# Hybrid decoder layer: ScalarE's order in the stick task, the fields' layout and requests, and who splits values in two stages

## Chip, cores and metric

One NeuronCore of a Trainium2 chip runs the whole layer as one launch. The metric is the device time in microseconds (us); 1,000 ns are 1 us. TensorE multiplies matrices, VectorE, ScalarE and GpSimd work on elements, SyncE's queue (SP) issues most DMA requests. In rows of the profile they are PE (PEld for its weight loads), DVE, ACT, POOL and SP.

## The reference

For 16 learned tokens followed by 1,024 others, all 1,024 wide, one layer is computed:

```
xn = RMSNorm(h);  P = xn @ W_in
A:  RWKV-7, 8 heads x 64: token shift, decay, gates, the scan
    S = S * w + (S @ -kk) (kk * a)^T + v k^T,   y = S r,  group norm, bonus, gate
B:  stick-breaking attention, 8 heads x 64, for s < t:
    z = q.k / sqrt(64)
    log A[t,s] = log_sigmoid(z[t,s]) + sum over s < j < t of (log_sigmoid(z[t,j]) - z[t,j])
    o = A @ v, RMSNorm per head
h += RMSNorm(concat(A, B) @ W_out)
h += RMSNorm(relu(RMSNorm(h) @ W_up)^2 @ W_down)
```

Since log_sigmoid(z) - z = -softplus(z), an exponent in B is z minus a running sum of softplus(z) over the keys between.

## The kernel before

The layer runs as stages, one after the other, with a barrier between them: the norm and transpose of x, the input projection (`stage_in_proj`), the two mixers together (`stage_mix`), the heads' norms (`stage_post_heads`), the output projection, and the feed-forward part. The change touches the middle three.

**High and low halves.** A large product of float32 values is made of three (or, with one exact side, two) products in the rounded type fp32r. Each operand is split: the high half is the value converted to fp32r, the low half is the value minus the high half. Whoever makes the high half and whoever makes the low half are named in the code by `high...` and `low...`.

**`stage_in_proj`** also prepares five fields for each of the four pairs of RWKV heads, cut into 17 chunks of 64 tokens, and stores them to `chunk_dram`; `F_A`, `F_R`, `F_B`, `F_K`, `F_V` give their places there (places 0 to 4).

**`stage_mix`** runs two independent computations interleaved on the same engines. The RWKV scan goes by laps, one lap a chunk, 18 laps of 8 slots each (`LAP_SLOTS`): in lap n the front half of chunk n and the rear half of chunk n - 1. A chain of small products of TensorE alternates with steps of VectorE (masked copies out of PSUM: `nb`, `xx`, `krk`, `zi`, `fv`, `qm`, `state`) and copies of ScalarE (`xx`, `xt`, `wu`, `nb`, `fv`, `y`). The chunk's fields are loaded by `load(n, s)` into `fld` (A, R, an identity that stays, B) and, with the halves of the partitions exchanged, into `swp` (A, R, K, V): six requests a chunk on SP's queue.

The sticks go by ticks. There are 124: 112 tasks (four pairs of heads, two heads, two groups of 512 queries, blocks of 128 keys; 64 tasks are 512 columns wide, 16 each 384, 256 and 128) and 12 turns that transpose v. Each engine runs its own list, a tick is cut into four quarters on each, and `program` deals the quarters out behind the slots of the laps, evenly. Every engine executes in order, so a quarter that waits holds up all that stands behind it, the lap's steps too. For task t the work is:

- TensorE, tick t, quarter 0: z into the one PSUM bank `zb` (2 products), after ScalarE has copied the z of t - 1 out
- ScalarE, tick t, quarter 2: the copy of z to SBUF (L1026)
- VectorE, tick t, quarter 3: w = min(z, 40) (L1149)
- ScalarE, tick t + 1, quarter 0: w = exp(w), w = ln(1 + w) (L1011, L1013)
- VectorE, tick t + 1, quarter 2: the maximum of z and w, which is softplus (L1142)
- GpSimd: on the diagonal blocks a mask (L915), then the high half (L934) and the low half (L936)
- TensorE, tick t + 3, quarter 3: the running sum (`tri`, 2 products, or one for a narrow task)
- VectorE, tick t + 4, quarter 0: the exponent, z minus the sum (L1130)
- ScalarE, tick t + 5, quarter 1: exp of it, the weights (L1019); GpSimd masks them on the diagonal
- TensorE, ticks t + 5 and t + 6: `rest` (2 products) and the product of two heads' weights with v

The first requests of the stage are: v of pair 0, the six of chunk 0, q and k of pair 0 in four (part 0), the six of chunk 1, q and k in four more (part 1), v of pair 1. Before the first tick's end ScalarE needs part 0 and part 1 (`high_q`, `high_k`).

**`stage_post_heads`** takes the mean and variance of y over each head with TensorE (`ones_bd`), ScalarE makes 1/sqrt as exp(-0.5 ln), VectorE applies norm, bonus and gate for the four pairs, and then the norm of o. Beside it `w_out` is split for the next stage, eight tiles of 128x1024: high halves by VectorE (L1470) between the first norm step and the rest, low halves by GpSimd (L1490). Four of the tiles (`w_raw`) are already there, four (`w_rest`) are loaded in the stage, behind the bonus and gate of pair 0. Bonus and gate have two buffers: SP loads those of pair q once pair q - 2 is gated.

## Time and profile before

| | us |
|---|---|
| median of 3 timed runs (lowest to highest) | 1727.83 (1727.64 to 1730.01) |
| the profiled execution | 1725.34 |
| its span, first to last instruction | 1723.6 |
| PE, DVE, ACT, POOL busy in the span | 1566.2, 816.3, 696.6, 513.2 |
| stage_mix, first request to last instruction (378.4 to 840.5) | 462 |
| stage_post_heads (840.8 to 894.3) | 53 |

The first three lines measure the same kernel; the profiled execution lies 2.5 us under the median. Busy times are sums of the durations of an engine's instructions; in the sum for PE a product counts until its result has landed, so a PE that is shown busy isn't at its peak.

### The profile page before, as it was taken

What the parts mean: (1) busy time and instruction counts of PE and PEld (TensorE: products, weight loads), DVE (VectorE), ACT (ScalarE), POOL (GpSimd) and SP (SyncE); (2) the same over time, 40 slices, a digit from 0 to 9 for tenths busy, and PEclk for the clock granted to TensorE, in tenths of its full rate; (3) what the DMA queues carried; (4) which work ended last, traced back from release to release, by engine and by line L of the source; (5) the groups of instructions that cost most, each with busy time, mean ns of one, the idle gap of its engine ahead of it and who ended that gap; (6) DMA issues with size and microseconds to landing.
All of it is one profiled execution on the core that took longest, in us unless ns stands there. A gap on an engine that the chain in (4) does not pass through costs nothing. (4 is left out here: it accounts for less than half of the span.)

```text
span 1723.6 us, 38309 instructions
## 1 busy us (share of the span) xinstructions
PE 1566.2 (91%) x15700; PEld 1307.7 (76%) x15700; DVE 816.3 (47%) x1125; ACT 696.6 (40%) x1231; POOL 513.2 (30%) x523
## 2 busy tenths in 40 slices
PE   4999999976988889889919959999999999999997
PEld 3999999965676666767508848888888888888886
DVE  5133433324666667666663434444444444444436
ACT  5144534415777677667723432222222222222213
POOL 6432343322545355454533431111111111111110
PEclk7999999987999999999959979999999999999999
DMA  3334354463512323111331232111111111111104
GB/s 133 115 127 159 131 203 148 153 185 71 144 46 61 71 55 77 46 46 25 99 85 73 86 111 73 49 49 49 49 49 49 49 49 49 49 49 49 61 0 171
DMA packets 81570, 143.98 MB, mean 84 GB/s; under 512 B 15632, under 2 KB 51472, under 8 KB 81440
## 3 DMA queue, kind: packets, MB, share of 16 engines
q1 hardware_dynamic: 77696, 128.26, 24.3%
q10 hardware_dynamic: 3744, 13.85, 2.0%
q8 instruction: 99, 1.62, 0.4%
q14 instruction: 31, 0.25, 0.0%
HBM read 104.51 MB, written 37.57 MB: 82 GB/s over the span
## 5 line engine op out<-in xcount | busy, mean ns | idle before, releaser
L1816 POOL TENSOR_TENSOR ffn_ul<-ffn_relu,ffn_uh 128x512 fp32r<-128x512 f32 x64 | 82.8, 1294 | 575.8 <-ACT ffn_uh L1788 575.8
L1845 DVE TENSOR_TENSOR all_acc<-all_acc,ffn_down 128x512 f32<-128x512 f32 x240 | 161.1, 685 | 122.1 <-PE ffn_down L1892 121.5
L618 PE MATMUL inproj_acc<-xn_xh,inproj_wh 128*128 128x346 f32 (+1 forms) x624 | 207.6, 333 | 8.4 <-DVE inproj_wl L539 8.4
L1884 PE MATMUL ffn_up<-all_mh,ffn_wuh 128*128 128x512 f32 x512 | 200.2, 391 | 11.3 <-DVE ffn_wul L1828 11.3
L618 PE MATMUL inproj_acc<-xn_xh,inproj_wl 128*128 128x346 f32 (+1 forms) x624 | 201.2, 322 | 0.0
L618 PE MATMUL inproj_acc<-xn_xl,inproj_wh 128*128 128x346 f32 (+1 forms) x624 | 201.2, 322 | 0.0
L1892 PE MATMUL ffn_down<-ffn_wdh,ffn_uh 128*128 128x512 f32 x512 | 200.0, 391 | 0.0
L1884 PE MATMUL ffn_up<-all_ml,ffn_wuh 128*128 128x512 f32 x512 | 199.9, 390 | 0.0
L1884 PE MATMUL ffn_up<-all_mh,ffn_wul 128*128 128x512 f32 x512 | 199.9, 390 | 0.0
L1892 PE MATMUL ffn_down<-ffn_wdh,ffn_ul 128*128 128x512 f32 x512 | 199.4, 389 | 0.0
L1892 PE MATMUL ffn_down<-ffn_wdl,ffn_uh 128*128 128x512 f32 x512 | 199.2, 389 | 0.0
L1836 DVE TENSOR_TENSOR ffn_relu<-ffn_relu 128x512 f32<-128x512 f32 x64 | 44.3, 692 | 218.9 <-ACT ffn_relu L1786 218.9
L1780 ACT ACTIVATE ffn_wdh<-ffn_raw_d 128x1024 fp32r<-128x1024 f32 x32 | 32.2, 1052 | 266.7 <-PE ffn_down L1892 265.4
L618 PEld LDWEIGHTS inproj_acc<-xn_xh,inproj_wh 128*128 128x128 f32 x624 | 117.9, 189 | 12.1 <-ACT inproj_wh L472 8.8
L1884 PEld LDWEIGHTS ffn_up<-all_mh,ffn_wuh 128*128 128x128 f32 x512 | 96.6, 189 | 31.8 <-DVE ffn_wul L1828 11.7
L618 PEld LDWEIGHTS inproj_acc<-xn_xl,inproj_wh 128*128 128x128 f32 x624 | 118.0, 189 | 3.3 <-issue 1.9
L1786 ACT ACTIVATE ffn_relu<-ffn_up 128x512 f32<-128x512 f32 x64 | 38.3, 599 | 203.0 <-PE ffn_up L1884 203.0
L618 PEld LDWEIGHTS inproj_acc<-xn_xh,inproj_wl 128*128 128x128 f32 x624 | 118.1, 189 | 0.0
L936 POOL TENSOR_TENSOR mix_wsl<-mix_w,mix_wsh 128x512 fp32r<-128x512 f32 (+2 forms) x96 | 111.8, 1165 | 8.0
L1892 PEld LDWEIGHTS ffn_down<-ffn_wdh,ffn_uh 128*128 128x128 f32 x512 | 96.1, 188 | 22.1 <-DVE all_acc L1845 2.6
L1884 PEld LDWEIGHTS ffn_up<-all_ml,ffn_wuh 128*128 128x128 f32 x512 | 96.7, 189 | 20.1
L1884 PEld LDWEIGHTS ffn_up<-all_mh,ffn_wul 128*128 128x128 f32 x512 | 96.5, 189 | 20.1
(251 smaller groups left out, 3383.0 us busy)
## 6 DMA issues: line engine op xcount, KB each, us to landing
ffn_raw_u<-in_w_up SPq DMA_DIRECT2D x32, 512.0 KB, 3.3
ffn_raw_d<-in_w_down SPq DMA_DIRECT2D x32, 512.0 KB, 4.3
xn_raw<-in_w_in SPq DMA_DIRECT2D x28, 512.0 KB, 4.8
p_scratch<-inproj_out ACTq DMA_DIRECT2D x26, 520.0 KB, 2.7
chunk_scratch<-inproj_fields SPq DMA_DIRECT2D x4, 2720.0 KB, 9.2
mix_swp<-chunk_scratch SPq DMA_DIRECT2D x68, 128.0 KB, 3.6
inproj_rkv<-p_scratch SPq DMA_DIRECT2D x14, 520.0 KB, 4.4
mix_fld<-chunk_scratch SPq DMA_DIRECT2D x17, 256.0 KB, 3.0
```

The source lines that it names most:

```text
L618: last = pe.matmul(acc[g][:, 0:size], w[s][:, kt, :], xx[:, kt, col:col + size], start=(kt == 0 and j == 0), stop=(kt == KD - 1 and j == 2))
L936: pool.tensor_tensor(low, part, high.bitcast(F32), ALU.subtract).then_inc(soft_low.sem, 1)
L1780: act.activation(wdh[s][:, f, :], raw_d[f][:, :], ACT.Copy).then_inc(wd_high.sem, 1)
L1786: act.activation(relu[j % 2][:, :], ups[j][:, :], ACT.Relu).then_inc(relu_done.sem, 1)
L1816: pool.tensor_tensor(ul[s][:, f, cols], relu[j % 2][:, :], uh[s][:, f, cols].bitcast(F32), ALU.subtract).then_inc(u_low.sem, 1)
L1836: dve.tensor_tensor(relu[j % 2][:, :], relu[j % 2][:, :], relu[j % 2][:, :], ALU.mult).then_inc(squared.sem, 1)
L1845: dve.tensor_tensor(part, part, downs[o % 4][:, :], ALU.add).then_inc(added.sem, 1)
L1884: last = pe.matmul(ups[j][:, :], w[f][:, k, :], xx[:, k, cols], start=(k == 0 and jj == 0), stop=(k == KD - 1 and jj == 2))
L1892: last = pe.matmul(downs[o % 4][:, :], u[s][:, f, t * P:(t + 1) * P], w[s][:, f, g * 512:g * 512 + 512], start=(first and f == 0 and jj == ...
```

## The change

Five edits. (1) **Layout and requests**: the fields' places become B, A, R, K, V, so that `fld` takes one request (B, A, R) and each half of `swp` one (A, R, K, V): three requests a chunk. At the start the fields of chunk 0 come ahead of v, and part 1 of q and k ahead of chunk 1. (2) **Start**: the sticks get no quarter in the first two slots, and are dealt out over the other 142. (3) **ScalarE**: in a tick the exp of the weights is now in quarter 0, the copy of z in quarter 1, and exp and ln of the task before in quarter 2. (4) **VectorE**: in a tick the exponent (quarter 0); in quarter 1 the low half of task t - 3 in GpSimd's place, and then the minimum of task t - 1 (before: of t, in quarter 3); in quarter 2 the maximum of task t - 2 (before: t - 1). The low halves of q and k move from quarter 1 to quarter 3. GpSimd keeps the masks and the high halves. (5) **Norm stage without GpSimd**: VectorE makes the high halves of the first four tiles as a multiplication by 1.0 and their low halves right behind; ScalarE copies the other four, ahead of its logarithms, and VectorE makes their low halves behind the four pairs' gates, ahead of the norm of o.

```diff
-F_A, F_R, F_B, F_K, F_V = range(5)
+F_B, F_A, F_R, F_K, F_V = range(5)
+SB_START = 2
-X_A, X_R, X_I, X_B = range(4)
+X_B, X_A, X_R, X_I = range(4)
...
-                    due = k * quarters // slots
+                    due = max(0, k - SB_START) * quarters // (slots - SB_START)
...
-                sp.dma_start(both(fld[s][:, :, X_A:X_I, :]), src[:, :, 0:2 * CH]).then_inc(loaded[s], 16)
-                sp.dma_start(fld[s][:, :, X_B, :], src[:, :, 2 * CH:3 * CH]).then_inc(loaded[s], 16)
+                sp.dma_start(both(fld[s][:, :, X_B:X_I, :]), src[:, :, 0:3 * CH]).then_inc(loaded[s], 16)
                 for h in range(2):
-                    sp.dma_start(both(swp[s][hs[1 - h], :, Y_A:Y_K, :]), src[hs[h], :, 0:2 * CH]).then_inc(loaded[s], 16)
-                    sp.dma_start(both(swp[s][hs[1 - h], :, Y_K:, :]), src[hs[h], :, 3 * CH:]).then_inc(loaded[s], 16)
+                    sp.dma_start(both(swp[s][hs[1 - h], :, :, :]), src[hs[h], :, CH:]).then_inc(loaded[s], 16)
...
+            load(0, 0)
             load_values(0)
-            load(0, 0)
             load_part(0, 0)
+            load_part(0, 1)
             load(1, 1)
-            load_part(0, 1)
...
# GpSimd, sticks
-                        part, high, low = soft_of(t), wsh[t % 4][:, off:], wsl[t % 4][:, off:]
+                        part, high = soft_of(t), wsh[t % 4][:, off:]
                         pool.tensor_copy(high, part).then_inc(soft_high.sem, 1)
-                        soft_high.wait(pool, t)
-                        pool.tensor_tensor(low, part, high.bitcast(F32), ALU.subtract).then_inc(soft_low.sem, 1)
...
# ScalarE, sticks: these lines move from quarter 0 to quarter 2
                     t = now - 1
                     if is_task(t):
                         part = w[t % 3][:, at(t).off:]
                         clamped.wait(act, t)
                         act.activation(part, part, ACT.Exp).then_inc(exp_done.sem, 1)
                         exp_done.wait(act, t)
                         act.activation(part, part, ACT.Ln, bias=1.0).then_inc(ln_done.sem, 1)
...
# VectorE, sticks, quarters 1 to 3
+                    t = now - 3
+                    if is_task(t):
+                        soft_high.wait(dve, t)
...
+                            high, low = wsh[t % 4][:, at(t).off:], wsl[t % 4][:, at(t).off:]
+                            dve.tensor_tensor(low, soft_of(t), high.bitcast(F32), ALU.subtract).then_inc(soft_low.sem, 1)
+                    t = now - 1
+                    if is_task(t):
+                        off = at(t).off
+                        z_copied.wait(dve, t)
+                        soft_low.wait(dve, t - 3)
+                        dve.tensor_scalar(w[t % 3][:, off:], z[t % 4][:, off:], SB_CLAMP, None, ALU.min).then_inc(clamped.sem, 1)
                     yield
-                    t = now - 1
+                    t = now - 2
                     if is_task(t):
                         ln_done.wait(dve, t)
...
-                    t = now
-                    if is_task(t):
-                        off = at(t).off
-                        z_copied.wait(dve, t)
-                        soft_low.wait(dve, t - 3)
-                        dve.tensor_scalar(w[t % 3][:, off:], z[t % 4][:, off:], SB_CLAMP, None, ALU.min).then_inc(clamped.sem, 1)
...
# stage_post_heads, ScalarE
+            act.wait_ge(w_loaded, 16 * (KD // 2))
+            for k in range(KD // 2, KD):
+                act.activation(wh[:, k, :], w_tile(k), ACT.Copy).then_inc(w_rest_high, 1)
# stage_post_heads, VectorE
-            for k in range(KD):
-                if k == KD // 2:
-                    dve.wait_ge(w_loaded, 16 * (KD // 2))
-                dve.tensor_copy(wh[:, k, :], w_tile(k)).then_inc(w_high, 1)
+            for k in range(KD // 2):
+                dve.tensor_scalar(wh[:, k, :], w_tile(k), 1.0, None, ALU.mult).then_inc(w_high, 1)
+            for k in range(KD // 2):
+                dve.wait_ge(w_high, k + 1)
+                low_of(k)
...
+            for k in range(KD // 2, KD):
+                dve.wait_ge(w_rest_high, k - KD // 2 + 1)
+                low_of(k)
```

`low_of(k)` is the subtraction that GpSimd made before, as a `tensor_tensor` of VectorE; GpSimd has no program in that stage any more.

## Rows read from the trace of the kernel before

**Rows 1.** Windows: busy time of each engine, granted clock, DMA share, GB/s
```profile
core 0: us, PE busy (x) PEld busy (x) DVE busy (x) ACT busy (x) POOL busy (x), PEclk, DMA share, GB/s
392.00:394.00 2.00, 0.00 (x0) 0.00 (x0) 1.30 (x2) 1.96 (x3) 0.00 (x0) 0.50 1.24 207
402.00:841.00 439.00, 391.35 (x9983) 304.52 (x9984) 279.81 (x552) 311.24 (x651) 212.80 (x320) 0.98 0.24 58
```

**Rows 2.** Waits of PE in 402 to 832 us: total, times, longest
```profile
PE mix_zb L1322 <- ACT mix_z L1026: 25.2, 37, 1.8
PE mix_bank L1176 <- DMA mix_swp<-chunk_scratch: 7.5, 7, 2.1
PE mix_bank L1176 <- ACT mix_xx L978: 4.1, 5, 1.3
PE mix_bank L1176 <- DVE mix_zi L1093: 3.4, 6, 1.4
```

**Rows 3.** Waits of ACT in 402 to 832 us
```profile
ACT mix_w L1011 <- DVE mix_w L1149: 65.4, 70, 3.3
```

**Rows 4.** Timeline of ACT and of DVE, one wide tick: start, duration, [idle before]
```profile
778.94 0.63 ACT L1011 ACTIVATE mix_w<-mix_w 128x512 f32<-128x512 f32 x1 [0.71 <-DVE mix_w L1149]
...
778.26 0.64 DVE L1149 TENSOR_SCALAR mix_w<-mix_z 128x512 f32<-128x512 f32 x1 [0.31 <-ACT mix_z L1026]
```

**Rows 5.** Timeline of POOL: the high halves of the first and the twelfth wide task
```profile
753.50 0.73 POOL L934 CAST mix_wsh<-mix_w 128x512 fp32r<-128x512 f32 x1
...
796.65 0.61 POOL L934 CAST mix_wsh<-mix_w 128x512 fp32r<-128x512 f32 x1 [3.10 <-DVE mix_w L1142]
```

**Rows 6.** Groups by form, 378 to 843 us: busy, mean ns, idle before
```profile
L1142 DVE TENSOR_TENSOR mix_w<-mix_z,mix_w 128x512 f32<-128x512 f32 x64 | 49.4, 772 | 30.5 <-ACT mix_w L1013 30.5
L1130 DVE TENSOR_TENSOR mix_a<-mix_z,mix_cb 128x512 f32<-128x512 f32 x64 | 43.4, 679 | 4.9 <-PE mix_cb L1307 4.8
L1149 DVE TENSOR_SCALAR mix_w<-mix_z 128x512 f32<-128x512 f32 x64 | 39.4, 615 | 17.4 <-ACT mix_z L1026 16.8
L1065 DVE TENSOR_TENSOR mix_nb<-mix_bank,early_masks 128x512 f32<-128x512 f32 x17 | 11.8, 692 | 25.1 <-PE mix_bank L1176 17.5 <-issue 7.6
...
L1082 DVE COPY mix_fv<-mix_bank 128x256 f32<-128x256 f32 x17 | 7.2, 422 | 14.2 <-PE mix_bank L1176 14.2
...
L936 POOL TENSOR_TENSOR mix_wsl<-mix_w,mix_wsh 128x512 fp32r<-128x512 f32 x64 | 84.1, 1314 | 5.3
```

**Rows 7.** Timelines of POOL and of DVE: a low half and a minimum together
```profile
792.27 1.28 POOL L936 TENSOR_TENSOR mix_wsl<-mix_w,mix_wsh 128x512 fp32r<-128x512 f32 x1
...
792.50 1.33 DVE L1149 TENSOR_SCALAR mix_w<-mix_z 128x512 f32<-128x512 f32 x1 [0.99 <-ACT mix_z L1026]
```

**Rows 8.** Timelines of SP and of ACT: the stage's start
```profile
392.68 0.61 SPq L870 DMA_DIRECT2D mix_k<-p_scratch  x1
...
400.85 1.06 ACT L998 ACTIVATE mix_qh<-mix_q 128x1024 fp32r<-128x1024 f32 x1 [6.89 <-DMA mix_k<-p_scratch]
```

**Rows 9.** The tile mixed_wh: ns min/median/max, first and last start
```profile
L1470 DVE CAST mixed_wh<-early_w_raw x4: 685/1772/2861, 849.1 to 853.1; 128x1024 fp32r<-128x1024 f32 x4
```

**Rows 10.** Timelines of DVE and of ACT in the norm stage
```profile
849.13 6.84 DVE L1470 CAST mixed_wh<-early_w_raw 128x1024 fp32r<-128x1024 f32 x4
855.89 11.15 DVE L1470 CAST mixed_wh<-post_w_rest 128x1024 fp32r<-128x1024 f32 x4
...
873.62 1.22 DVE L1480 TENSOR_TENSOR mixed_y<-post_dev,post_gate 128x1024 f32<-128x1024 f32 x1
...
882.16 1.28 DVE L1478 SCALAR_TENSOR_TENSOR post_dev<-post_dev,post_vec,post_bonus 128x1024 f32<-128x1024 f32 x1 [2.34 <-DMA post_gate<-gate_scratch]
...
889.41 4.86 DVE L1483 SCALAR_TENSOR_TENSOR mixed_o<-mixed_o,post_vec,post_ors 128x1024 f32<-128x1024 f32 x4
...
850.21 1.10 ACT L1450 ACTIVATE post_rs<-post_sums,post_eps 128x1024 f32<-128x1024 f32 x1
851.34 1.06 ACT L1452 ACTIVATE post_rs<-post_rs 128x1024 f32<-128x1024 f32 x1
```

More of the change, by code:

```diff
@@ L1006, in sticks @@
                 for now in range(N + SB_LAG + 1):
-                    t = now - 1
-                    if is_task(t):
-                        part = w[t % 3][:, at(t).off:]
-                        clamped.wait(act, t)
-                        act.activation(part, part, ACT.Exp).then_inc(exp_done.sem, 1)
-                        exp_done.wait(act, t)
-                        act.activation(part, part, ACT.Ln, bias=1.0).then_inc(ln_done.sem, 1)
-                    yield
                     t = now - 5
@@ L1033, in sticks @@
                                        zb[:, 0:TURNS * P].rearrange("p (b n) -> p b n", n=P), ACT.Copy).then_inc(z_copied.sem, 1)
+                    yield
+                    t = now - 1
+                    if is_task(t):
+                        part = w[t % 3][:, at(t).off:]
+                        clamped.wait(act, t)
+                        act.activation(part, part, ACT.Exp).then_inc(exp_done.sem, 1)
+                        exp_done.wait(act, t)
+                        act.activation(part, part, ACT.Ln, bias=1.0).then_inc(ln_done.sem, 1)
                     yield
@@ L1103, in rear @@
                 MG.wait(dve, m, "y", 1)
-                VG.done(dve.tensor_tensor(qm[:, :, :, :], by2(bank[2]), fld[s][:, :, X_R:X_B, :], ALU.add), "qm")
+                VG.done(dve.tensor_tensor(qm[:, :, :, :], by2(bank[2]), fld[s][:, :, X_R:, :], ALU.add), "qm")
                 yield "qm"
@@ L1131, in sticks @@
                     yield
-                    if now - 1 in split_at:
-                        low_q(*split_at[now - 1])
-                    if now - 2 in split_at:
-                        low_k(*split_at[now - 2])
+                    t = now - 3
+                    if is_task(t):
+                        soft_high.wait(dve, t)
+                        if at(t).narrow:
+                            dve.sem_inc(soft_low.sem, 1)
+                        else:
+                            high, low = wsh[t % 4][:, at(t).off:], wsl[t % 4][:, at(t).off:]
+                            dve.tensor_tensor(low, soft_of(t), high.bitcast(F32), ALU.subtract).then_inc(soft_low.sem, 1)
+                    t = now - 1
+                    if is_task(t):
+                        off = at(t).off
+                        z_copied.wait(dve, t)
+                        soft_low.wait(dve, t - 3)
+                        dve.tensor_scalar(w[t % 3][:, off:], z[t % 4][:, off:], SB_CLAMP, None, ALU.min).then_inc(clamped.sem, 1)
                     yield
-                    t = now - 1
+                    t = now - 2
                     if is_task(t):
@@ L1143, in sticks @@
                     yield
-                    t = now
-                    if is_task(t):
-                        off = at(t).off
-                        z_copied.wait(dve, t)
-                        soft_low.wait(dve, t - 3)
-                        dve.tensor_scalar(w[t % 3][:, off:], z[t % 4][:, off:], SB_CLAMP, None, ALU.min).then_inc(clamped.sem, 1)
+                    if now - 1 in split_at:
+                        low_q(*split_at[now - 1])
+                    if now - 2 in split_at:
+                        low_k(*split_at[now - 2])
                     yield
@@ L1399, in stage_post_heads @@
         (mean_done, var_done, osum_done, dev_done, dev_squared, o_squared, rs_ln, rs_done, ors_ln, ors_done,
-         scaled, with_bonus, gated, o_scaled, w_high, w_low) = (m.sem(name) for name in (
+         scaled, with_bonus, gated, o_scaled, w_high, w_rest_high, w_low) = (m.sem(name) for name in (
             "mean_done", "var_done", "osum_done", "dev_done", "dev_squared", "o_squared", "rs_ln", "rs_done", "ors_ln",
-            "ors_done", "scaled", "with_bonus", "gated", "o_scaled", "w_high", "w_low"))
+            "ors_done", "scaled", "with_bonus", "gated", "o_scaled", "w_high", "w_rest_high", "w_low"))
         block = ctx.enter_context(nc.Block())
@@ L1484, in _ @@
                                          ALU.mult, ALU.mult).then_inc(o_scaled, 1)
-        @block.gpsimd
-        def _(pool):
-            for k in range(KD):
-                pool.wait_ge(w_high, k + 1)
-                pool.tensor_tensor(wl[:, k, :], w_tile(k), wh[:, k, :].bitcast(F32),
-                                   ALU.subtract).then_inc(w_low, 1)
 def stage_out_proj(nc, y_sb, o_sb, wh, wl, x_dram, gain_row, gain_cols, ident, h_dram, mh, ml):
```

5 lines of the change are left out of this document (3 added, 2 removed).

## Prediction

> **What bounds the kernel now.** I read the windows first, stage by stage. Both changed stages stand between barriers, so what each of them saves or loses goes straight into the total. In stage_mix, from 402 to 841 us, PE is shown busy 391.4 of 439 us, ACT 311.2, DVE 279.8 and POOL 212.8 [rows 1]: PE is nearest to its limit, and idle for 48 us. PE's waits say where from: 25.2 us of it before the product of z, which waits until ScalarE has copied the previous z out of the one bank; 7.5 us for the fields of a chunk; 4.1 and 3.4 us for the lap's steps on ScalarE and VectorE [rows 2]. So the z copy is late. Why, ScalarE's own waits tell: 65.4 us, in 70 pieces, before its exp for VectorE's minimum [rows 3]. The timeline of one wide tick shows the ring: VectorE's minimum starts 0.31 us idle after the copy of z (778.26), and ScalarE's exp after 0.71 us idle (778.94) [rows 4]; the next copy of z stands behind that exp on ScalarE. Copy, minimum, exp, ln, exp of the weights, next copy are in series, though the engines are free for a third of the time. A wide tick takes 3.92 us: from the first to the twelfth wide task of a group, (796.65 - 753.50) / 11 [rows 5].
>
> In stage_post_heads VectorE sets the end. Its eight high halves hold it from 849.13 to 867 [rows 10]. One that ran alone took 0.685 us, the longest 2.861 [rows 9]. ScalarE's first 1/sqrt, which the next VectorE step needs, was done at 852.4 (851.34 + 1.06) [rows 10].
>
> **The change, part by part.**
>
> *Start of stage_mix.* Before, the last request of part 1 of q and k starts at 392.68 and lets ScalarE's high_q go at 400.85; ScalarE stood idle for 6.89 us until then, with the lap's steps behind it [rows 8]. The DMA engines were saturated, at 207 GB/s [rows 1]. Part 1 now goes ahead of chunk 1, which is 384 KB of `fld` and 512 KB of `swp`, 0.92 MB: 4.4 us at that rate. Three requests fewer ahead of it, at 0.61 us each on SP [rows 8], count only where SP and not the transfer is behind; I add 0.6, one such issue. So part 1 lands about 5 us earlier. Dealing no quarters in the first two slots lets two slots of the lap run while q and k are loading; a slot is 439 / 138 or some 3.2 us, of which about half is the lap's: 1.5 us. Sum -6.5 us; bounds -2 (all but the two slots and half a us lost) and -9.
>
> *ScalarE's order.* The copy of z now stands in front of exp and ln of the task before, and the minimum that these wait for is asked for a quarter earlier on VectorE and isn't of the z just copied. The ring is open. PE's 25.2 us [rows 2] go if nothing takes their place. I count all of it here and what takes its place under VectorE.
>
> *Requests.* Three a chunk instead of six save 3 x 0.61 = 1.8 us of issue before each chunk's last landing; PE waited 7.5 us in 7 laps, 1.1 us each [rows 2]: -6 us, bounds -2 and -7.5.
>
> *VectorE in the sticks.* It gains the low halves: like L1130, 679 ns wide [rows 6], so 64 x 0.68 = 43.5, and by columns 16 x (384 + 256) more at 1.33 ns a column or 13.6: 57 us. It gets back what GpSimd's low halves cost it. The minimum averaged 615 ns [rows 6], and one that started 0.23 us into a low half took 1.33 us and ended with it [rows 7]; alone it should take 430 ns, as a one-source step of twice the columns took 685 alone [rows 9]: 64 x 0.18 = 12, and 64 x (772 - 690) = 5 of the maximum (690 by L1130 and L1065 [rows 6]). Net +40: VectorE busy 320 of the 439 us it had, or of some 410 then, 78%. Per wide tick: low 0.68, exponent 0.68, minimum 0.43, maximum 0.69 and its share of the lap. The lap's twelve steps, from L1065 with 11.8 us to L1082 with 7.2 [rows 6], sum to 102 us, 6.0 a lap of 7.3 ticks, 0.8 a tick. Together 3.3 us. That is under 3.92, but the lap's steps on VectorE stand more often behind a stick. PE's waits for lap steps were 4.1 + 3.4 = 7.5 us [rows 2]; I let them and the new waits for low halves come to 9 us more. Bounds: 0 (VectorE had 159 us idle, more than it gains), and 29, half of the low halves' 57 us lying open.
>
> *GpSimd* loses 84.1 us of wide low halves [rows 6] and is on no path; its masks and high halves have three quarters of a tick between VectorE's maximum and the low half that needs them.
>
> *A rule weighed against the rows.* GpSimd's low half and VectorE's minimum above ended together, 0.23 us apart at the start [rows 7]. The Trainium skill, in "SBUF — State Buffer", section "Who interferes with whom", says that the two engines share one port pair as an exclusive lock, held for the whole instruction, and that VectorE competes for it in its fast one-source mode and with two sources in SBUF. By that rule, the trace agrees: the minimum waited the low half out. It would also speak against this change, as the new low half on VectorE has two sources in SBUF while GpSimd still converts; what that would cost is the slower rival below, worked out from rows.
>
> *Norm stage.* VectorE is through with the first norm step at 849.2; four high halves of 0.69 [rows 9] and four low halves of 1.2 (as the two-source step of 1.22 [rows 10]) end at 856.7. ScalarE is ready at 850.2 [rows 10] but now waits for the second four tiles, which had landed by 855.89, as VectorE's copy of them started then without a wait [rows 10]. I take 854, late in that interval, since they stand third in the queue. Four copies of about 1 us and one pair of ln and exp, 851.34 + 1.06 - 850.21 = 2.2, give the first 1/sqrt at 860.2. So this is what the first pair waits for, not VectorE. Three steps of 1.22 to 1.28 (the 3.3 us forms go with GpSimd) put the first gate at 864.0. Before, it was done at 874.84 (873.62 + 1.22) [rows 10]: -10.8. From there to the norm of o is 14.6 us (889.41 - 874.84), which includes waiting for the buffers of bonus and gate (2.34 us at 882.16 alone) [rows 10]; I leave it as it is, since SP asks for them when the gate is done. Four low halves of 1.2 come ahead of the norm of o: +4.8. Net -6.0; bounds -10 (tiles there at 850.2) and -4 (at 855.9).
>
> **Sum.** -6.5 - 25.2 - 6 + 9 - 6.0 = -34.7 us. The profiled execution took 1725.34, so 1690.6 for one like it. The median of the timed runs lies 2.5 above it and the lowest 2.3; a smaller part of that shift carries over than it seems from one execution, so I put the median at 1692.
>
> **Rivals.**
>
> *VectorE becomes the bound.* For it: 3.3 us of VectorE's work in a wide tick, in order, with waits for PE, POOL and ACT between, and every product of the lap behind it. If half of the low halves lie open (+29 instead of +9) and the z waits turn into waits for `xx`, `zi` and `tri`, -34.7 becomes about -15: 1712. Against it: VectorE's idle time in the stage is 159 us [rows 1].
>
> *More than PE's waits comes back.* Part of PE's busy time is landing time that shows only because the next product isn't there yet; with ScalarE 65.4 us freer, of which just 25.2 reach PE as waits, and VectorE +0 instead of +9, the wide tick could go to 3.3 us, 64 x 0.62 = 40 us instead of 25.2: -6.5 - 40 - 6 + 0 - 6 = -58, 1669. Against: PE's own work in a tick.
>
> *Slower: VectorE and GpSimd in a new ring.* Maximum, mask and high half on GpSimd, low half, minimum, next maximum are in series on two engines: 0.69 + 1.1 (a high half of 0.61 to 0.73 [rows 5], a mask of a quarter of its columns, taken at 0.3, and handovers) + 0.68 + 0.62, and if the exponent (0.68) and the lap's share (0.8) find no room in GpSimd's part, 4.6 us a wide tick. Then 64 x (4.6 - 3.92) = +43 in place of -25.2 and +9, and with -18.5 from start, requests and norm stage 1725.3 + 25 = 1750. It decides for slower from a tick of 3.92 + 18.5 / 64 = 4.2 us. This is where the lock of the skill's page would act: two-source steps and the minimum held up by GpSimd's 0.6 to 0.7 us high half. Against it: the exponent stands exactly between maximum and low half, and fills GpSimd's 1.1 us with 0.68 of work; the ring is then 3.5 us.
>
> *The change doesn't do what it says:* the z copy moves but PE waits as long for it, because ScalarE's exp of the weights ahead of it waits for the exponent, VectorE's quarter 0 behind `tri`. Then only start, requests and norm stage count, less the 9: about 1716. I take it with the first rival.
>
> **Chances.** Forecast (1680 to 1702) 0.52; VectorE the bound, or PE's wait kept (1702 to 1721) 0.22; more comes back (under 1680) 0.15; within 0.2% 0.04; slower ring 0.07. A measurement of this kernel tells a change from none at about 0.2% or 3.5 us. Faster 0.89, same 0.04, slower 0.07. The range, with the bounds of the start (+4.5, -2.5), of VectorE (+20, -9) and of the norm stage (+2, -4), is 1668 to 1714.
>
> **What would show it.** PE's wait for L1026 should fall from 25.2 to under 5 us and ScalarE's wait for the minimum from 65.4 to under 25; stage_mix should be 26 to 32 us shorter, its first copy of q's part 1 at about 396 instead of 400.85; no wait of PE for `swp` above 0.3 us a lap; the minimum near 0.43 us; the norm stage 47 us long with its first gate near 23 us after its start (before 34). Wrong steps would show as PE waiting for `zi`, `xx`, `krk` or `cb` by VectorE with 20 us or more, or VectorE waiting for POOL's L934. What would make the prediction wrong most surely is a wide tick of over 3.7 us.

## The result, and the profile after

| | before | after |
|---|---|---|
| median of the timed runs (lowest to highest), us | 1727.74 (1723.55 to 1730.01) | 1708.03 (1703.76 to 1712.22) |
| profiled execution, us | 1725.34 | 1703.76 |
| its span | 1723.6 | 1702.0 |
| stage_mix, first request to the norm stage's first instruction | 462 | 447 |
| stage_post_heads | 53.4 | 46.4 |

Four runs each; the ratio is 0.9882, with a 95% interval of 0.9855 to 0.991. The changed kernel is 1.2% faster, some 20 us, where I had forecast 35. The profiled execution of after is the lowest of its four runs, 4.3 us under their median, so its trace shows a little more gain than the timing does.

Window of after (columns as in [rows 1]): `stage_mix` from 402, as [rows 1].

```profile
402.00:825.00 423.00, 382.49 (x9847) 300.35 (x9841) 301.43 (x642) 308.97 (x642) 95.61 (x224) 1.00 0.25 58
```

GpSimd has given up 117 us and VectorE has gained 22. PE still stands idle for 423 - 382.5 = 40.5 us, hardly less than the 48 of before. Part of the gain lies ahead of 402 us, and part in the products themselves: over the whole stage (378 to 841 us before, 378 to 825 after) PE is idle for 54 us instead of 65, and busy for 393.2 instead of 397.9 with as many products, at a mean granted clock of 0.98 instead of 0.96. What PE waits for has changed, as the waits of PE in 402 to 816 us show beside [rows 2]:

```profile
PE mix_cb L1310 <- DVE mix_wsl L1135: 16.7, 23, 1.8
PE mix_bank L1180 <- DMA mix_swp<-chunk_scratch: 5.9, 5, 1.6
PE mix_bank L1180 <- issue: 3.3, 6, 0.7
PE mix_ob L1353 <- POOL mix_a L914: 3.1, 7, 1.1
PE mix_zb L1326 <- ACT mix_z L1014: 2.3, 5, 0.8
PE mix_bank L1180 <- DVE mix_zi L1089: 2.3, 4, 0.9
```

The wait for the copy of z has gone from 25.2 to 2.3 us. In its place stands a wait that wasn't there before: 16.7 us for VectorE's low half. The waits of ACT and of DVE in the same stretch (compare [rows 3]):

```profile
ACT mix_z L1014 <- DVE mix_a L1126: 27.8, 26, 3.6
ACT mix_w L1027 <- DVE mix_w L1141: 22.2, 31, 2.7
```
```profile
DVE mix_a L1126 <- PE mix_cb L1311: 20.1, 29, 1.9
DVE mix_wsl L1135 <- POOL mix_wsh L933: 8.8, 16, 1.0
```

ScalarE's wait for the minimum fell from 65.4 to 22.2. VectorE's own wide steps, groups by form in 378 to 825 us (compare [rows 6]):

```profile
L1135 DVE TENSOR_TENSOR mix_wsl<-mix_w,mix_wsh 128x512 fp32r<-128x512 f32 x64 | 44.7, 698 | 5.1 <-POOL mix_wsh L933 4.2
L1148 DVE TENSOR_TENSOR mix_w<-mix_z,mix_w 128x512 f32<-128x512 f32 x64 | 43.8, 684 | 0.0
...
L1141 DVE TENSOR_SCALAR mix_w<-mix_z 128x512 f32<-128x512 f32 x64 | 26.9, 420 | 0.0
```

The minimum takes 420 ns and not 615, the maximum 684 and not 772: VectorE got back what GpSimd's low halves had cost it.

Why is VectorE, busy for 301 of 423 us, late with a low half? The longest of these waits tells it. First the timeline of PE, then that of VectorE:

```profile
607.86 0.34 PE L1311 MATMUL mix_cb<-mix_wsl,mix_rest_r 128*128 128x384 f32 x1
609.95 0.50 PE L1310 MATMUL mix_cb<-mix_wsh,mix_tri_r 128*128 128x512 f32 x1 [1.75 <-DVE mix_wsl L1135]
```
```profile
607.01 0.69 DVE L1061 TENSOR_TENSOR mix_nb<-mix_bank,early_masks 128x512 f32<-128x512 f32 x1 [1.25 <-PE mix_bank L1180]
607.62 0.44 DVE L1063 COPY_PREDICATED mix_xx<-early_masks,mix_bank 128x256 f32<-128x256 uint32 x1
607.95 0.43 DVE L1065 COPY_PREDICATED mix_xx<-early_masks,mix_bank 128x256 f32<-128x256 uint32 x1
608.28 0.43 DVE L1089 COPY_PREDICATED mix_zi<-early_masks,mix_bank 128x256 f32<-128x256 uint32 x1
608.61 0.68 DVE L1126 TENSOR_TENSOR mix_a<-mix_z,mix_cb 128x512 f32<-128x512 f32 x1
609.21 0.69 DVE L1135 TENSOR_TENSOR mix_wsl<-mix_w,mix_wsh 128x512 fp32r<-128x512 f32 x1
```

VectorE idles 1.25 us for a product of the lap, then does four of the lap's steps and the exponent, and only then the low half, though GpSimd's high half had been there since 606.8. PE waits from 608.2 to 609.95. VectorE isn't full; it is in order, and the low half stands behind steps that wait.

The norm stage, timeline of VectorE (compare [rows 10]):

```profile
833.51 2.49 DVE L1478 TENSOR_SCALAR mixed_wh<-early_w_raw 128x1024 fp32r<-128x1024 f32 x4
835.92 4.63 DVE L1469 TENSOR_TENSOR mixed_wl<-early_w_raw,mixed_wh 128x1024 fp32r<-128x1024 f32 x4
844.02 1.28 DVE L1486 SCALAR_TENSOR_TENSOR post_dev<-post_dev,post_vec,post_rs 128x1024 f32<-128x1024 f32 x1 [3.48 <-ACT post_rs L1459]
...
846.66 1.22 DVE L1491 TENSOR_TENSOR mixed_y<-post_dev,post_gate 128x1024 f32<-128x1024 f32 x1
...
862.25 4.62 DVE L1469 TENSOR_TENSOR mixed_wl<-post_w_rest,mixed_wh 128x1024 fp32r<-128x1024 f32 x4
866.79 4.87 DVE L1497 SCALAR_TENSOR_TENSOR mixed_o<-mixed_o,post_vec,post_ors 128x1024 f32<-128x1024 f32 x4
```

The eight splitting steps of the first four tiles end at 840.5, and the next step waits 3.48 us for ScalarE, whose copies of the other four tiles had to wait 3.24 us for their loading (timeline of ACT):

```profile
837.93 3.90 ACT L1453 ACTIVATE mixed_wh<-post_w_rest 128x1024 fp32r<-128x1024 f32 x4 [3.24 <-DMA post_w_rest<-in_w_out]
```

### The profile page after: what moved, and what is told of

Read it like the earlier page. It is cut to its first block and busy times, and to the rows that moved or that the text cites. A ratio compares the mean times of both kernels' runs of the same rounds, so it can differ in the third digit from the quotient of the medians.

```text
span 1702.0 us, 38257 instructions
## 1 busy us (share of the span) xinstructions
PE 1565.4 (92%) x15700; PEld 1309.4 (77%) x15700; DVE 831.0 (49%) x1225; ACT 702.2 (41%) x1235; POOL 373.9 (22%) x419
## 2 busy tenths in 40 slices
DMA packets 63345, 143.97 MB, mean 85 GB/s; under 512 B 6112, under 2 KB 33248, under 8 KB 63216
## 5 line engine op out<-in xcount | busy, mean ns | idle before, releaser
L539 DVE TENSOR_TENSOR inproj_wl<-xn_raw,inproj_wh 128x1024 fp32r<-128x1024 f32 x27 | 33.1, 1227 | 165.5 <-ACT inproj_wh L472 165.5
L481 ACT ACTIVATE inproj_out<-inproj_acc 128x346 f32<-128x346 f32 (+1 forms) x78 | 35.7, 458 | 186.9 <-PE inproj_acc L618 186.9
L1891 PEld LDWEIGHTS ffn_up<-all_mh,ffn_wul 128*128 128x128 f32 x512 | 96.7, 189 | 20.2
```

The source lines that it names most:

```text
L481: group_read.done(act.activation(out[s][:, col:col + size], acc[g][:, 0:size], ACT.Copy), f"{g}")
L539: w_low.done(dve.tensor_tensor(wl[s][:, :, :], raw[s][:, :, :], wh[s][:, :, :].bitcast(F32), ALU.subtract), "all")
L1891: last = pe.matmul(ups[j][:, :], w[f][:, k, :], xx[:, k, cols], start=(k == 0 and jj == 0), stop=(k == KD - 1 and jj == 2))
```

## Experiments

Each kernel was run in five rounds beside the kernel before; times are medians, ratios are to the kernel before with their 95% intervals. 1708 us is the changed kernel. The kernel before had a median of 1728 to 1729 us in these rounds. A difference taken from two medians and one taken from two ratios can lie up to 2 us apart, and the intervals are 2 to 5 us to either side: smaller differences between two kernels are marked as not shown.

**Three parts alone.** First the norm stage, edit (5), with the rest as before.

```diff
-            for k in range(KD):
-                if k == KD // 2:
-                    dve.wait_ge(w_loaded, 16 * (KD // 2))
-                dve.tensor_copy(wh[:, k, :], w_tile(k)).then_inc(w_high, 1)
+            for k in range(KD // 2):
+                dve.tensor_scalar(wh[:, k, :], w_tile(k), 1.0, None, ALU.mult).then_inc(w_high, 1)
```

> The kernel before with the norm stage alone changed. Theory (each stage stands between barriers, gains add up): the norm stage takes 46.4 us from its first to its last VectorE step instead of 53.4, so the whole is 7 us or 0.4% faster and stage_mix is unchanged within 1 us. Rival (part of the 7 us comes from what the changed mix stage leaves behind, such as w_raw landed earlier or the clock): under 4 us.

Measured: 1721.33, ratio 0.996 (0.9945 to 0.9975), 7.9 us less than before by the medians, 6.9 by the ratio. The stage took 46.7 us, so the theory held for it. `stage_mix`, whose code is as before, took 2.4 us more in this trace than in the trace of before (464.9 and 462.5), where under 1 had been expected: two executions of the same code differ by that much.

Then the start and the requests, edits (1) and (2).

```diff
-                    due = k * quarters // slots
+                    due = max(0, k - SB_START) * quarters // (slots - SB_START)
...
-            load(1, 1)
             load_part(0, 1)
+            load(1, 1)
```

> The kernel before with the fields' layout, three requests a chunk, the new order of first requests and no sticks in the first two slots; engines' orders in a tick and the norm stage as before. Theory (the start saves 4.7 us, requests save little since a larger one lands later, 5.1 instead of 3.6 us): stage_mix 4 to 7 us shorter, 0.25 to 0.4% in all; PE's waits for swp from 402 us on stay at 5 to 8 us. Rival (fewer requests help the ring in each lap): 8 us or more, with waits for swp under 3 us.

Measured: 1725.61, ratio 0.998 (0.997 to 0.999): 3.6 us, not 12.5. Waits of PE, 402 to 832 us:

```profile
PE mix_zb L1321 <- ACT mix_z L1025: 29.1, 38, 2.4
...
PE mix_bank L1175 <- DMA mix_swp<-chunk_scratch: 3.3, 3, 1.4
```

The wait for `swp` did fall, from 7.5 to 3.3, but that for z rose by as much, from 25.2 to 29.1. And the first chunk was done 6.5 us earlier, just as forecast; at the last lap 0.6 us of it were left. The theory of 4 to 7 us for the stage failed in the trace, and so did its waits for `swp` of 5 to 8. PE's idle time in the whole stage did fall, from 65.1 to 60.7 us, but PE was busy for 402.3 us instead of 397.9 with as many products (378 to 841 us in both traces): what the waits gave back, longer products took.

Third, the sticks: edits (3) and (4) without the start.

```diff
# VectorE, quarter 1, and GpSimd's low half gone
+                            dve.tensor_tensor(low, soft_of(t), high.bitcast(F32), ALU.subtract).then_inc(soft_low.sem, 1)
```

> The kernel before with the sticks' part alone: ScalarE's and VectorE's new orders and the low half on VectorE. Theory (the z wait of 25 us is traded for some 20 us of waits for low halves and masks; lap steps and fuller engines give the rest): stage_mix 9 to 13 us shorter, PE's wait for the z copy under 5 us and for the low half 15 to 20 us. Rival (the sticks' part is worth nothing, all of the mix stage's gain is the start and the requests): within 3 us of before.

Measured: 1719.44, ratio 0.9954 (0.9936 to 0.9972): 9.8 us. PE waited 18.2 us for low halves and 4.8 for GpSimd's masks, 1.9 for z, as the theory had it; the stage was 7 us shorter in the trace (455.3 for 462.5), where 9 to 13 were expected. So the three parts are worth 7.9 + 3.6 + 9.8 = 21.3 us, and the whole 19.7. By the ratios it is 6.9 + 3.5 + 8.0 = 18.3 and 20.4. Within the intervals the parts add up.

**The requests alone**, edit (1) without the order of the start.

```diff
-                sp.dma_start(both(fld[s][:, :, X_A:X_I, :]), src[:, :, 0:2 * CH]).then_inc(loaded[s], 16)
-                sp.dma_start(fld[s][:, :, X_B, :], src[:, :, 2 * CH:3 * CH]).then_inc(loaded[s], 16)
+                sp.dma_start(both(fld[s][:, :, X_B:X_I, :]), src[:, :, 0:3 * CH]).then_inc(loaded[s], 16)
```

> The kernel before with the fields' layout and three requests a chunk alone; the order of the start and the slots stay. Theory A (the requests' issue was what PE waited for, as I predicted): PE's wait for swp, 7.5 us before, falls to 2 or less and the total by 4 to 6 us, to 1722 to 1724. Theory B (a larger request takes longer to land, 5.1 us in place of 3.6 in the changed kernel, and what PE doesn't wait for swp it waits for z or for VectorE): swp falls to some 3 us, the waits for z rise by as much, and the total is within 2 us of before.

Measured: 1727.60, ratio 0.9997 (0.9985 to 1.001): nothing. PE waited 4.4 us for `swp` (before 7.5) and 22.7 for z. Theory B's total, though not its rise of the z wait, which fell a little too. Other waits of PE, put down to "issue", rose from under 1 us to 6.5; why, the trace doesn't say. The packets under 512 bytes fell from 15,632 to 6,112, and a `swp` request landed 5.2 us after its issue (median; 5.1 in the changed kernel) where it had been 3.6 before.

**No free slots at the start**, in the changed kernel.

```diff
-SB_START = 2
+SB_START = 0
```

> The changed kernel with the sticks dealt out from the first slot on (SB_START 0). Theory (the two free slots only put stick work off, which is done later at the same price): within 2 us of the changed kernel, with lap 0's last step 4 to 7 us later and the end of stage_mix the same. Rival (they fill the wait for q and k with lap work): 2 to 4 us slower.

Measured: 1705.39, ratio 0.9871 (0.985 to 0.9891), not slower than with them, and with overlapping intervals not shown to be faster either. The first chunk was done 4.8 us later in the profiled execution, as the theory said, but the stage didn't end at the same time: `stage_mix` took 452.0 us in this trace, and 447.0 in that of the changed kernel. The timed runs don't show these 5 us.

**ScalarE's order undone.** The changed kernel, but exp and ln of the task before are again in ScalarE's quarter 0, ahead of the copy of z:

```diff
+                    t = now - 1
+                    if is_task(t):
+                        part = w[t % 3][:, at(t).off:]
+                        clamped.wait(act, t)
+                        act.activation(part, part, ACT.Exp).then_inc(exp_done.sem, 1)
...
                     t = now - 5
...
                         exponent.wait(act, t)
```

> The changed kernel with one part undone: ScalarE goes back to exp and ln of the task before in quarter 0 and the copy of z behind them (quarter 2 of its list, behind the exp of the weights). VectorE keeps its new order and its low halves. Theory A (ScalarE's order is what took away PE's wait for the copy of z): with VectorE's minimum in quarter 1 the exp in quarter 0 now waits for it every tick, and the copy of z stands behind; PE's wait for the z copy goes from 2.3 back to 25 us or more, the stage is 25 to 45 us longer, 1733 to 1753 in all, slower than the kernel before. Theory B (moving the minimum off the z just copied opened the ring alone): ScalarE's order counts for little, PE's z wait stays under 8 us and the time is 1708 to 1714.

Measured: 1811.68, ratio 1.0476 (1.0457 to 1.0495), 104 us slower than the changed kernel. The direction is Theory A's; the size is more than twice what it allowed. This is not the order of before: there VectorE made the minimum in quarter 3 of the tick ahead, and here it makes it in quarter 1 of the tick in whose quarter 0 ScalarE already waits for it. So the run shows what two orders that don't fit cost, and that the minimum's new place needs the exp's new place with it; it does not measure what the old order alone had cost. Waits of PE and of ACT, 402 to 931 us, and the window of that stretch:

```profile
PE mix_zb L1326 <- ACT mix_z L1022: 67.2, 52, 2.7
PE mix_cb L1310 <- DVE mix_wsl L1135: 12.4, 19, 1.6
```
```profile
ACT mix_w L1007 <- DVE mix_w L1141: 181.1, 94, 6.5
```
```profile
402.00:931.00 529.00, 424.49 (x9866) 323.13 (x9865) 305.13 (x642) 305.67 (x643) 101.73 (x224) 0.92 0.20 47
```

In 402 to 824 us the changed kernel has PE busy for 382.5 of 422. Here it is 424.5 of 529: 65 us more of idle time, and 42 more of busy time for the same products. The second part goes with the granted clock, 0.92 where it was 1.00. Three neighbouring windows show it: PE busy throughout at full clock; then busy for only 1.49 of 4 us, with a wait of 2.4 us for z, behind which the clock falls; and then a stretch at a mean of 0.65, so mostly at 1.2 and not 2.4 GHz. Below them stands the product of z that ended the wait, 0.79 us long, where this form takes 0.44 on average in the changed kernel:

```profile
850.00:854.00 4.00, 4.00 (x102) 3.21 (x94) 3.39 (x7) 0.94 (x2) 0.61 (x1) 1.00 0.01 4
854.00:858.00 4.00, 1.49 (x15) 0.82 (x5) 3.43 (x7) 2.93 (x6) 0.61 (x1) 0.92 0.00 0
858.00:862.00 4.00, 4.00 (x84) 3.12 (x82) 1.35 (x3) 2.37 (x5) 0.03 (x1) 0.65 0.00 0
```
```profile
857.38 0.79 PE L1326 MATMUL mix_zb<-mix_qh,mix_ks 128*128 128x512 f32 x1 [2.42 <-ACT mix_z L1022]
```

An estimate of the clock's part: a mean of 0.92 is 0.16 of the time at the half level, 85 of 529 us; PE was busy for 0.8 of that, 68 us, which at full clock would have been 34. So the clock accounts for some 34 of the 42 us.

The Trainium skill, "TensorE: Matmul & The Clock Gate", Part 1, says that the gate follows how busy the engine has been. These windows agree: 1.00 before the wait of 2.42 us, 0.65 after it.

**VectorE's low halves left out.** The changed kernel with the 96 low halves of the tasks of 512, 384 and 256 columns not computed (the tiles hold zero, so the running sum lacks its low part); PE makes its products with them as before.

```diff
-                            high, low = wsh[t % 4][:, at(t).off:], wsl[t % 4][:, at(t).off:]
-                            dve.tensor_tensor(low, soft_of(t), high.bitcast(F32), ALU.subtract).then_inc(soft_low.sem, 1)
+                            dve.sem_inc(soft_low.sem, 1)
```

> The changed kernel without the 112 less 16 low halves of wide and middle tasks on VectorE: they are left out (the tiles hold zero from the start of the stage, so the running sum lacks its low part), and PE still makes its product with them. It measures what the 57 us of low halves on VectorE cost in all. Theory A (what I predicted: 9 us of them come through, the rest is hidden): 1708 less 9, 1699, and PE's waits fall by no more than 9. Theory B (what the missing 15 us of the sum are): PE's wait for the low half (16.7 us) goes and nothing takes its place, 1708 less 16 to 25, 1683 to 1692. Theory C (GpSimd's high half and masks, or PE itself, are next in line): PE's wait for the low half goes, but PE's waits for z, masks and steps of the lap, or its busy time in the stage, rise, and the total falls by less than 5.

Measured: 1687.07, ratio 0.9771 (0.9752 to 0.9789): 21 us less than the changed kernel, or 19 by the difference of the two ratios. The total and the low half's wait are Theory B's. Waits of PE, 402 to 816 us:

```profile
PE mix_bank L1181 <- DMA mix_swp<-chunk_scratch: 6.4, 6, 1.4
PE mix_ob L1354 <- POOL mix_a L914: 4.4, 8, 1.3
PE mix_zb L1327 <- ACT mix_z L1014: 3.9, 9, 0.8
```

The wait for low halves is gone, and the others rose by no more than 1.6 us each. This is the size of what the low halves on VectorE cost, 19 to 21 us where 9 were forecast.

**Low halves back on GpSimd**, with the new orders of ScalarE and VectorE kept.

```diff
# GpSimd
                         pool.tensor_copy(high, part).then_inc(soft_high.sem, 1)
+                        soft_high.wait(pool, t)
+                        pool.tensor_tensor(low, part, high.bitcast(F32), ALU.subtract).then_inc(soft_low.sem, 1)
```

> The changed kernel with the low halves back on GpSimd, all else as changed. Theory A (PE's new wait is for the low half because VectorE makes it behind the exponent, which itself waits for PE): PE's waits for the low half fall from 16.7 to under 6 us and the whole is 5 to 12 us faster than the changed kernel, 1.6 to 1.9% faster than before. Theory B (GpSimd's 1.3 us low half holds the minimum and the maximum up and is itself too slow): as slow as the changed kernel or up to 10 us slower, minimum back at a mean of 600 ns or more.

Measured: 1713.55, ratio 0.9912 (0.9895 to 0.9929), 5 us slower than the changed kernel, with intervals that overlap a little. Waits of PE, and two groups of VectorE and one of GpSimd, 402 to 816 us:

```profile
PE mix_ob L1348 <- POOL mix_a L914: 14.3, 15, 2.0
...
PE mix_cb L1305 <- POOL mix_wsl L935: 5.2, 6, 1.4
```
```profile
L1143 DVE TENSOR_TENSOR mix_w<-mix_z,mix_w 128x512 f32<-128x512 f32 x62 | 50.5, 814 | 0.3 <-ACT mix_w L1032 0.3
...
L1136 DVE TENSOR_SCALAR mix_w<-mix_z 128x512 f32<-128x512 f32 x63 | 36.1, 573 | 0.2 <-ACT mix_z L1017 0.2
```
```profile
L935 POOL TENSOR_TENSOR mix_wsl<-mix_w,mix_wsh 128x512 fp32r<-128x512 f32 x61 | 79.6, 1305 | 5.1
```

The wait for low halves fell from 16.7 to 5.2 us, but GpSimd's masks of the weights, queued behind a low half of 1.3 us, took its place: 14.3 us. Theory A had the wait right and the total wrong; the total and the direction are Theory B's. This run also shows the new orders without the move of the low halves: 1729.3 less 7.9 (norm stage) and 3.6 (start) less 1713.6 leaves some 4 us for them, an amount no larger than its uncertainty, though PE's wait for z had fallen to 3.6 us. And VectorE's minimum and maximum rose again, from 420 and 684 to 573 and 814 ns. The Trainium skill, "SBUF — State Buffer", section "Who interferes with whom", says that VectorE and GpSimd share one port pair, held by one at a time. The minimum of 615, 420 and 573 ns with, without and again with GpSimd's low halves agrees.

**The low half earlier on VectorE.** In the changed kernel the low half stands behind the exponent. First ahead of it:

```diff
# VectorE, quarter 0: the blocks in this order
+                    (low half of t = now - 3)
                     (exponent of t = now - 4)
                     yield
-                    (low half of t = now - 3)
                     (minimum of t = now - 1)
```

> The changed kernel with one swap on VectorE: the low half of task t - 3 stands in quarter 0, ahead of the exponent of task t - 4, not behind it. Theory A (a ring: the exponent waits for PE's running sum, 20.1 us, the low half stands behind it, and PE waits for the low half, 16.7 us): PE's wait for the low half falls under 8 us, and the whole is 5 to 10 us faster than the changed kernel, 1.5 to 1.8% faster than before. Theory B (VectorE is late because it has too much to do, or because GpSimd hands the high half over late, 8.8 us): the wait for the low half stays at 14 us or more or comes back as VectorE waiting for GpSimd's high half, and the time is within 3 us of the changed kernel.

Measured: 1712.41, ratio 0.9914 (0.9893 to 0.9935), 4 to 5 us slower than the changed kernel, with intervals that overlap; in the trace its `stage_mix` is 8 us longer. Waits of VectorE and of ScalarE, 402 to 816 us:

```profile
DVE mix_wsl L1128 <- POOL mix_wsh L933: 48.6, 62, 1.1
```
```profile
ACT mix_z L1014 <- DVE mix_a L1134: 56.3, 56, 4.1
```

PE's wait for low halves fell from 16.7 to 8.1 us. But VectorE now stood idle 48.6 us for GpSimd's high half (8.8 before), and ScalarE 56.3 for the exponent (27.8 before), so PE's wait for z came back, 7.3 us. Theory A's faster kernel did not come; the idle time for GpSimd is what Theory B had named. Then low half and minimum both ahead of the exponent:

```diff
+                    (low half of t = now - 3)
+                    (minimum of t = now - 1)
+                    yield
                     (exponent of t = now - 4)
                     yield
-                    (low half of t = now - 3)
-                    (minimum of t = now - 1)
```

> The changed kernel with the low half and the minimum in quarter 0 on VectorE and the exponent in quarter 1. Theory A: as the swap of the low half alone, and ScalarE's exp waits less for the minimum (22.2 us before the swap), but its copy of z more for the exponent (27.8 us): 3 to 10 us faster than the changed kernel. Theory B: within 3 us of it, or slower by up to 5 us as the copy of z is late again.

Measured: 1717.82, ratio 0.9939 (0.9918 to 0.9961), 10 us slower than the changed kernel, twice what Theory B allowed. ScalarE waited 76.7 us for the exponent and PE 14.6 for z. The exponent is what fills GpSimd's time, and the order of the changed kernel has the lowest time of the three.

**Norm stage: ScalarE's copies behind its logarithms.**

```diff
-            act.wait_ge(w_loaded, 16 * (KD // 2))
-            for k in range(KD // 2, KD):
-                act.activation(wh[:, k, :], w_tile(k), ACT.Copy).then_inc(w_rest_high, 1)
...
                 act.activation(rs[q], rs[q], ACT.Exp, scale=-0.5).then_inc(rs_done, 1)
+            act.wait_ge(w_loaded, 16 * (KD // 2))
+            for k in range(KD // 2, KD):
+                act.activation(wh[:, k, :], w_tile(k), ACT.Copy).then_inc(w_rest_high, 1)
```

> The changed kernel with ScalarE's four copies of w_out behind the first four pairs of ln and exp in the norm stage. Theory (VectorE's 3.48 us wait for the first 1/sqrt is there because the copies, and the tiles' landing, stand ahead of it): that wait falls to 0 and the norm stage is 3 to 4 us shorter, 43 instead of 46.4, or 0.2% of the whole. Rival (the buffers of bonus and gate set the end of the four gates): under 1 us.

Measured: 1705.42, ratio 0.9879 (0.9852 to 0.9906). By the medians that is 2.6 us less than the changed kernel, by the ratios 0.5, so a gain of the whole is not shown. The stage itself took 43.0 us instead of 46.4 in the trace, as the theory said, and VectorE's first norm step follows its low halves without a wait:

```profile
836.91 4.62 DVE L1469 TENSOR_TENSOR mixed_wl<-early_w_raw,mixed_wh 128x1024 fp32r<-128x1024 f32 x4
841.45 1.28 DVE L1486 SCALAR_TENSOR_TENSOR post_dev<-post_dev,post_vec,post_rs 128x1024 f32<-128x1024 f32 x1
```

**Both amendments together**: the late copies of the run above, and no free slots.

```diff
-SB_START = 2
+SB_START = 0
```

> The changed kernel with both amendments that cost nothing: ScalarE's copies of the four w tiles behind its ln and exp pairs in the norm stage, and no free slots at the start. Theory A (the two parts are in stages apart and each is worth its own measure, -3 and 0 to -3): 1703 to 1706, the norm stage 43 us. Rival (the start's five us are given back within the stage, and only the norm stage counts): 1705 to 1708 and stage_mix no shorter than in the changed kernel.

Measured: 1703.63, ratio 0.9856 (0.9835 to 0.9876), the fastest median of all kernels that compute the whole, 4 us under the changed kernel; but the intervals overlap, so it is not shown to be faster than it. The time is in Theory A's range, but the trace is the rival's: `stage_mix` took 451.8 us, again 5 us more than in the changed kernel (447.0).

**Where in stage_mix the time went.** From the timeline of VectorE: the first and the last `state` step start at, for example, 422.70 and 823.99 in after; the stage's first request is at 378.30. The first one closes chunk 0, in the second of the 18 laps; 16 laps follow to the last. One execution each; the same code (`stage_mix` of before, in the run with the norm stage alone) differs by 2.4 us between two of them.

| kernel | first chunk done, us | the 16 laps after it, us |
|---|---|---|
| before | 56.0 | 405.2 |
| requests alone | 55.4 | 405.7 |
| start and requests | 49.5 | 411.1 |
| sticks alone | 53.3 | 400.7 |
| after | 44.4 | 401.3 |
| after, no free slots | 49.2 | 401.5 |
| after, low halves on GpSimd | 43.7 | 412.8 |
| after, low half first | 43.8 | 410.2 |
| after, low halves left out | 43.4 | 385.0 |

The 16 laps gain 3.9 us in the changed kernel, little more than two executions differ by, and 20.2 with VectorE's low halves left out.

## Why the prediction came out as it did

The forecast was 1692 with a range of 1668 to 1714; measured 1708. The sign, the opening of the ring and the range held. (The bounds that I named for the range add up to 1676 to 1718; 1708 lies in either.) But it lies outside the forecast's own 1680 to 1702, to which I gave 0.52, and in the 1702 to 1721 of "VectorE the bound, or PE's wait kept", to which I gave 0.22. The size fell short by 15 us, and two terms of the sum account for it. It showed first in the length of stage_mix, 15 us shorter in the trace where I had named 26 to 32.

- **z wait, -25.2**: right as a wait. It fell to 2.3 us, and with ScalarE's old order behind VectorE's new one it is 67. How much time its going gives depends on what stands next in line. With the low halves left on GpSimd the new orders gave some 4 us, as PE then waited 14.3 us for masks. With no low halves at all the opened ring is worth somewhat more than 25.2: before less the kernel without low halves is 41.9 us, less 7.9 (norm stage) and 3.6 (start) leaves 30, more than the 25.2 us of z waits. VectorE's minimum and maximum got back 64 x (0.195 + 0.088) = 18 us from GpSimd in this; how much of it reached PE wasn't measured by itself.
- **VectorE and the new waits, +9**: mis-sized, and the larger error. The low halves cost 19 to 21 us when taken out, and PE's waits for them and for GpSimd's masks, 16.7 + 3.1, say the same. I had summed VectorE's work in a wide tick, 3.3 of 3.92 us, and taken the slack for cover. The parts of that sum came out well (low half 698 ns for 680, minimum 420 for 430, maximum 684 for 690). But what PE waits for is not how much VectorE does; it is what stands in front of the low half in its order: the exponent, and behind a wait of its own the lap's steps. VectorE was busy for 312 of the stage's 447 us, close to the 320 foretold. My bound of 29, half of the low halves lying open, was about as far off on the other side as my value of 9: some third of them lay open. So the rival "VectorE becomes the bound", 1712 with its +20 on top of the 9, came nearer to 1708 than my 1692, but partly by luck: it took 29 for the low halves and left the start's and the requests' terms at their full size. The sign that I had named, 20 us of PE's waits for VectorE, was just missed: 16.7 for the low half, 2.3 for `zi`, 0.2 for `krk`.
- **Start, -6.5, and requests, -6**: mis-sized; together 3.6 us measured, the requests none. The landings were right: q's part 1 went at 396.11 for 396 foretold, and the first chunk was done 6.5 us earlier. But in the run with start and requests alone the 16 laps after it took 5.9 us longer. Being early with laps is worth little while something else sets the pace; that this is the ticks of the sticks is my reading, and no run shows it apart from the longer products of that trace (402.3 us of PE's busy time for 397.9). And PE's 7.5 us for `swp` was no separate cost: where it fell to 3.3 the wait for z rose by as much, and with the requests alone it gained no time. In the changed kernel it still stood at 5.9 us, 0.35 a lap for the 0.3 I had named. In the trace of after the first chunk led the sticks alone by 8.9 us (44.4 for 53.3), and 8.3 of it stayed to the end (445.7 for 454.0); the timed runs put start and requests at 3.5 there too (1719.4 - 7.9 - 1708.0). The profiled execution of after lies 4.3 us under its median, which is most of the gap; which of the two is nearer stays open.
- **Norm stage, -6.0**: right; -7.9 timed, -7.0 in the trace. ScalarE's copies began 12.7 us into the stage (13.1 foretold), the first gate ended at 22.6 (23.1 foretold), the whole took 46.4 us (47 foretold). That ScalarE's copies, not VectorE, would hold the first norm step was right too, and moving them takes 3.4 us off the stage.
- **GpSimd, on no path**: nearly. PE waited 3.1 us for its masks and VectorE 8.8 for its high halves, the sign I had named for the slower ring. That ring didn't set the pace, because the exponent fills GpSimd's part; where the exponent was moved out of it, VectorE's wait rose to 48.6 us. Nor did GpSimd's high halves slow VectorE's low halves much: they took 698 ns where I had put 680.
- **The wide tick.** From the first to the twelfth wide task of a group it took (783.35 - 742.91) / 11 = 3.68 us, for 3.92 before [rows 5] and 3.40 without low halves ((766.52 - 729.17) / 11). I had said 3.7 would break the forecast; it came within 0.02 of that. Twelve tasks of one group are a small sample, in which single steps between two high halves range from 2.3 to 5.2 us. Timeline of POOL in after:

```profile
742.91 0.61 POOL L933 CAST mix_wsh<-mix_w 128x512 fp32r<-128x512 f32 x1
...
783.35 0.61 POOL L933 CAST mix_wsh<-mix_w 128x512 fp32r<-128x512 f32 x1 [3.67 <-DVE mix_w L1148]
```

With the runs' values the sum is -3.6 - 30 + 21 - 7.9 = -20.5, and 19.7 were measured. (The 30 is worked out from the same run as the 21, so this closes the sum but is no second proof of it.) By part, without that run, it is 21.3.

## What to carry to other kernels

Where engines run in order, what an operation that moves to another engine costs the path is set less by its duration than by its place (here 19 to 21 us for 57 us of work, on an engine that was idle for three tenths of the stage): look at what stands in front of it there, whether that waits itself, and who needs the result; idle time of the engine is no sure cover for it. A wait that goes gives back only what the next one in line leaves. A stall that shows beside a longer one, like `swp` beside z here, is not a term to be subtracted by itself. And a stage needn't gain at its end what it gains at its start: 6.5 us became 0.6.

## What was not expected of the hardware

- ScalarE's old order beside VectorE's new one cost 104 us where 25 to 45 were expected. 65 us of it were PE's idle time and 42 PE's busy time at a granted clock of 0.92 for 1.00: with 52 waits before z, up to 2.7 us long and 67 us in all, the products between them took longer too.
- Halving the number of requests for the same bytes gained nothing, and each of the larger ones (256 KB for 128) took longer to land, 5.1 to 5.2 us for 3.6.
- ScalarE's and VectorE's copies of a 128x1024 tile stood at 3.90 and 2.49 us for four, 0.98 and 0.62 each; VectorE's as a multiplication by 1.0, beside no other engine's work on SBUF, where its plain copies took 1.77 (median) beside GpSimd's [rows 9]. Whether the form or the neighbour made the difference no run tells: a plain copy took 0.685 at best.
